# Sum of squares of a head tile: one float32 product against two products of a tile split in two rounded parts

## What is computed

```python
def rmsnorm_2(x, g):
    xf = x.astype(jnp.float32)
    y = xf * lax.rsqrt(jnp.mean(xf * xf, axis=-1, keepdims=True) + EPS)
    return (y * g.astype(jnp.float32)).astype(x.dtype)

# in each of two layers, HEAD_DIM = DIFF_QK_DIM = 64:
h = rmsnorm_2(x, g_attn[l])
proj = jnp.einsum('bsd,dc->bsc', h, w_in[l])
qa, ka, va, qb, kb, vb = jnp.split(proj, offs, axis=-1)
qa = apply_rope(rmsnorm_2(qa.reshape(B, S, SWA_Q_HEADS, HEAD_DIM), qn_a[l]), cos_a, sin_a)
ka = apply_rope(rmsnorm_2(ka.reshape(B, S, SWA_KV_HEADS, HEAD_DIM), kn_a[l]), cos_a, sin_a)
ya = windowed_gqa_sink(qa, ka, va, sink[l])
qb = apply_rope(rmsnorm_2(qb.reshape(B, S, 2 * DIFF_HEADS, DIFF_QK_DIM), qn_b[l]), cos_b, sin_b)
kb = apply_rope(rmsnorm_2(kb.reshape(B, S, 2 * DIFF_HEADS, DIFF_QK_DIM), kn_b[l]), cos_b, sin_b)
yb = diff_attention(...)
```

## Time and profile before

| | |
|---|---|
| median of 3 runs | 2851.36 us (2851.34 to 2852.1) |
| span of the profiled execution | 2849.4 us |
| TensorE (PE), busy | 2816.4 us, 99% |
| weight loads (PEld), busy | 2362.2 us, 83% |
| VectorE (DVE), busy | 1709.0 us, 60% |
| ScalarE (ACT), busy | 1207.7 us, 42% |
| GpSimd (POOL), busy | 59.0 us, 2% |
| granted TensorE clock | 0.999 of full speed over the span |

### The profile page before, as it was taken

The page is one execution under the profiler, slowest core; times in us unless marked ns, Lnnn a source line. Parts: engine busy times, 40 slices in busy tenths (PEclk is TensorE's granted clock), DMA queues, the critical chain, the costliest instruction groups (busy, mean ns, idle before and its releaser), DMA issues.

```text
span 2849.4 us, 36896 instructions
## 1 busy us (share of the span) xinstructions
PE 2816.4 (99%) x14238; PEld 2362.2 (83%) x14238; DVE 1709.0 (60%) x2648; ACT 1207.7 (42%) x1860; POOL 59.0 (2%) x115
## 2 busy tenths in 40 slices
PE   8999999999999999999999999999999999999999
PEld 6998899999999976788888876588888766688887
DVE  5837768754674465447546467865365478765463
ACT  4236645321333384445334346653233455643231
POOL 0000000000000000000000010000000010000000
PEclk9999999999999999999999999999999999999999
DMA  7631023433432120022222232122223321123223
GB/s 289 229 96 30 16 97 107 133 131 100 132 122 72 59 76 16 1 78 97 98 94 99 94 109 70 32 84 99 94 96 106 101 87 49 49 97 105 92 100 103
DMA packets 73486, 266.16 MB, mean 93 GB/s; under 512 B 8816, under 2 KB 11376, under 8 KB 72032
## 3 DMA queue, kind: packets, MB, share of 16 engines
q1 hardware_dynamic: 63360, 230.31, 24.2%
q0 software_dynamic: 9952, 33.50, 3.5%
HBM read 253.55 MB, written 2.10 MB: 90 GB/s over the span
## 4 chain that ended last, share of the span: by engine, by line
PE 92%; DVE 3%; ACT 2%; issue 2%; DMA 0%; SPq 0%; ACTq 0%; DVEq 0%
PE psum L767 76%; PE psum L1142 2%; ACT temps L1419 2%; PE psum L1364 1%; PE psum L1302 1%; DVE row_stats L1988 1%; DVE arena L1988 1%; PE psum L1150 1%; PE psum L1170 1%; PE psum L1247 1%; PE psum L1229 1%; PE psum L1284 1%; PE psum L861 1%; PE psum L860 1%; PE psum L862 1%
## 5 line engine op out<-in xcount | busy, mean ns | idle before, releaser
L767 PE MATMUL psum<-arena_r,w_hi 128*128 128x512 f32 (+1 forms) x7416 | 2006.0, 369 | 2.5 <-DVE arena_r L1988 1.8
L767 PEld LDWEIGHTS psum<-arena_r,w_hi 128*128 128x128 f32 x7416 | 1336.8, 188 | 221.8 <-issue 61.8
L767 PE MATMUL psum<-arena_r,w_lo 128*128 128x512 f32 (+1 forms) x3708 | 1219.2, 364 | 0.0
L1988 DVE TENSOR_TENSOR w_lo<-w_raw,w_hi 128x1024 fp32r<-128x1024 f32 (+4 forms) x377 | 455.3, 1208 | 525.8 <-ACT w_hi L1419 525.2
L767 PEld LDWEIGHTS psum<-arena_r,w_lo 128*128 128x128 f32 x3708 | 682.3, 188 | 82.2
L1419 ACT ACTIVATE w_hi<-w_raw 128x1024 fp32r<-128x1024 f32 (+4 forms) x377 | 392.6, 1042 | 538.0 <-DMA w_raw<-in_weights 537.7
L1419 ACT ACTIVATE temps<-temps 128x512 f32<-128x512 f32 (+2 forms) x208 | 137.2, 662 | 154.9 <-DVE temps L1988 153.0
L1988 DVE SCALAR_TENSOR_TENSOR temps<-psum,vectors,temps 128x511 f32<-128x511 f32 x246 | 151.0, 655 | 63.5 <-ACT temps L1419 61.6
L1419 ACT ACTIVATE arena<-psum 128x768 f32<-128x768 f32 (+2 forms) x166 | 106.7, 647 | 172.3 <-PE psum L767 58.6
L1419 ACT ACTIVATE arena_r<-temps 128x512 fp32r<-128x512 f32 (+1 forms) x103 | 70.7, 687 | 141.1 <-DVE temps L1988 141.1
L1419 ACT ACTIVATE temps<-psum,vectors 128x768 f32<-128x768 f32 (+1 forms) x85 | 75.2, 885 | 118.5 <-PE psum L767 107.2
(11 more groups left out here) (226 smaller groups left out, 2249.4 us busy)
## 6 DMA issues: line engine op xcount, KB each, us to landing
w_raw<-in_weights SPq DMA_DIRECT2D x261, 512.0 KB, 3.3
w_raw<-in_weights SPq DMA_DIRECT2D x64, 704.0 KB, 4.1
arena<-in_ada SPq DMA_DIRECT2D x32, 512.0 KB, 3.6
arena<-in_ada POOLq DMA_DIRECT2D x24, 512.0 KB, 4.6
modulation_weights<-in_ada POOLq DMA_DIRECT2D x24, 512.0 KB, 3.9
arena<-in_ada_first SPq DMA_DIRECT2D x8, 1024.0 KB, 19.4
w_raw<-in_weights SPq DMA_DIRECT2D x32, 256.0 KB, 2.6
modulation_weights<-arena POOLq DMA_DIRECT2D x60, 128.0 KB, 1.9
```

What stands on the lines that cost most here:

```text
L767: last = mm(lin_at(t, segs, slots, upper)[:, s:s + m], w[:, c], x(k, s, m), start=(k == 0 and a == 0), stop=(k == n_k - 1 and a == 2))
L1988: op(*args, **kw).then_inc(*C.out(signal))
```

## The change

In a norm tile the squares are split like other numbers. ScalarE's square stays as it is. ScalarE then copies it into the rounded format (`square_high`, two pieces of 256 columns in the unused positions of temps), signal tail_hi. GpSimd subtracts the high part from the square and writes the low part over the square, in the rounded format (`square_low`), signal tail_lo. TensorE computes the sum by two products in the rounded format with a rounded copy of `blk`, the high part and then the low part, added in PSUM. The rounded views of temps and of the fixed constants are laid over the old ones; the copy of `blk` is made once, early in ScalarE's program.

With it the order moves: in tiles 1 to 8 the tail (of both kinds) stands behind k=6 instead of k=3, ScalarE does the weights (`ahead`) before the roots, and on GpSimd the swap of tile n-1 stands behind the subtract of tile n.

```diff
@@ build @@
+        T = as_loaded.enter_context(nc.sbuf_tensor("temps", [P, 6, NT], F32))
+        CF = as_loaded.enter_context(nc.sbuf_tensor("fixed_constants", [P, C_FIX], F32))
         as_loaded.close()
         AR = sb("arena_r", [P, ARENA], F32R)
         WL = sb("w_lo", [P, RING], F32R)
+        TR = sb("temps_r", [P, 6, NT], F32R)
+        CR = sb("fixed_r", [P, C_FIX], F32R)
         WH = sb("w_hi", [P, RING], F32R)
         X = sb("X", [P, DT, NT])
-        T = sb("temps", [P, 6, NT])
         SQSUM = sb("square_sum", [P, NT])
-        CF = sb("fixed_constants", [P, C_FIX])
...
+        def square_high(n):
+
+            return TR[:, 2 * (n % 2):2 * (n % 2) + 2, NX:NT]
+
+        def square_low(n):
+            return TR[:, n % 2, 0:NX]
@@ gpsimd @@
+            def low_square(n):
+
+                pool.wait_ge(*C.next("tail_hi"))
+                pool.tensor_tensor(halves(square_low(n)), halves(T[:, n % 2, 0:NX]), square_high(n).bitcast(F32),
+                                   ALU.subtract).then_inc(*C.out("tail_lo"))
+
...
                 for n in range(18):
-                    if specs[n].get("rope") is not None:
-                        swap(specs[n]["rope"], MLA_TAILS + 18 * l + n + 1, turned)
+                    if specs[n]["kind"] == "norm":
+                        low_square(n)
+                    if n and specs[n - 1].get("rope") is not None:
+                        swap(specs[n - 1]["rope"], MLA_TAILS + 18 * l + n, turned)
                         turned += 1
@@ tensor @@
-            ident, ones, blk = CF[:, C_ID:C_ID + P], CF[:, C_ONE:C_ONE + P], CF[:, C_BLK:C_BLK + P]
+            ident, ones, blk = CF[:, C_ID:C_ID + P], CF[:, C_ONE:C_ONE + P], CR[:, C_BLK:C_BLK + P].bitcast(F32)
+            blk_r = CR[:, C_BLK:C_BLK + P]
...
                 def tail(n):
 
-                    pe.wait_ge(sems["free_a"], first + n + 1)
                     if n:
                         taken_from(n - 1)
                     if specs[n]["kind"] == "norm":
-                        last = mm(PS[:, 0, :], blk, T[:, n % 2, 0:NX], start=True, stop=True)
+                        pe.wait_ge(*C.next("tail_lo"))
+                        mm(halves(PS[:, 0, :]), blk_r, square_high(n), start=True, stop=False)
+                        last = mm(PS[:, 0, :], blk_r, square_low(n), start=False, stop=True)
                     else:
+                        pe.wait_ge(sems["free_a"], first + n + 1)
                         for t in range(4):
...
-                        if n and k == (3 if p is None else 5):
+                        if n and k == (6 if p is None else 5):
                             tail(n - 1)
@@ scalar @@
             norm(ALL, mod_shift(0, 0), splits=((-1, 1), (0, 2), (5, 3)))
             load_set(SILU_SET)
+            step(CR[:, C_BLK:C_BLK + P], CF[:, C_BLK:C_BLK + P], ACT.Copy, "act_own")
...
                     step(T[:, n % 2, 0:NX], T[:, 2 + n % 2, 0:NX], ACT.Square if specs[n]["kind"] == "norm" else ACT.Copy, "free_a")
+                    if specs[n]["kind"] == "norm":
+                        step(square_high(n), halves(T[:, n % 2, 0:NX]), ACT.Copy, "tail_hi", after=C.at("free_a"))
...
                 for n in range(1, 18):
                     squared(n - 1)
                     p = band_step(n)
+                    ahead()
                     if p is None:
                         tail_root(n - 1)
-                    ahead()
```

More of the change, by code:

```diff
@@ L506, in build @@
             tail_sum tail_rs tail_made rot_in0 rot_in1 kpe_in rope_made down_taken key_taken v_done v_even v_odd up_taken lat_sq lat_sum kpe_squared cn_done kpe_made
-            nm_made e_made p_made tp_done pt_made pv_done factor_made y_scaled y_hi y_done od_made
+            tail_hi tail_lo nm_made e_made p_made tp_done pt_made pv_done factor_made y_scaled y_hi y_done od_made
             lam_in lam_sum lam_exp sub_rs zero_made raw_hi raw_done raw_scaled dve_gate""".split()
```

## The result

The changed kernel takes 2883.55 us (2882.46 to 2884.06, 4 runs) beside 2851.73 for the kernel before (2851.34 to 2852.16, 4 runs): ratio 1.0112, 95% interval 1.01 to 1.0124. Forecast were 2839.4 us. The profiled span is 2881.7 us.

The account below looks back on a forecast made before the run. TensorE, busy 99% of the 2849.4 us span, was taken as the bound. Cheaper tails (-11.7), the first tails' wait (-0.5) and a startup copy (+0.2) gave 2837.4, plus 1.96 outside the span 2839.4 us; range 2838.5 to 2848.

Parts of the forecast that it names:

- What would show it: Signs in the changed kernel's timeline: 1.13 us between w_lo products across a tail, period 5.9, TensorE waiting under 1 us.
- Price of the tail: On TensorE, each of 26 square-sum tails falls from 0.90 to 0.45 us, saving 11.7 us in all.
- Period of a tile: TensorE's time for 24 products and one tail falls from 6.35 us to 5.89.
- The sum: Span 2849.4 - 11.7 - 0.5 + 0.2 = 2837.4 us; with the 1.96 around it 2839.4 us.
- The layer's first tail: TensorE's old wait at each layer's first tail goes and nothing replaces it: 0.5 us gained over two layers.
- The subtract: GpSimd's subtract for the low part takes an estimated 1.4 us, ending a microsecond before the early tails: no cost.
- Rival 1: GpSimd's subtract starved by VectorE's dense runs, tails wait, 21 us lost: 2860 us; chance 0.08 full, 0.08 in part.
- Rival 2: GpSimd's subtract slow by itself: over 2.5 us early tails wait; 2843.6 us at 2.8, 2852 at 3.4; chance 0.05.
- rival 3: ScalarE's extra 0.6 us in the banded-attention tiles ends up on the path, 7.2 us: 2846.6 us; chance 0.04.
- Rival 4: The rounded product in two pieces costs a float32 pass, so nothing is saved: 2851 us; chance 0.03.

Follow-up runs that it names:

- e2: The kernel before with 32 unused bytes per partition in front of w_hi, moving w_hi and all tensors behind it: 2893.33 us.
- e4: The kernel before with only the change's allocation, temps and fixed constants in front of w_hi: 2893.37 us.
- e5: The changed kernel with w_hi directly behind w_lo, at its address in the kernel before: 2839.81 us.
- e15: The changed kernel with w_hi at its old address and the split undone (one float32 product, no copy or subtract), new order kept: 2851.07 us.
- e9: The kernel before with 32 unused bytes between arena and w_lo, so w_lo and w_hi both move against the arena: 2888.72 us.
- e16: The kernel before with w_lo 32 bytes further from the arena and w_hi 256 bytes further: 2904.3 us.
- e13: The changed kernel with w_hi at its old address and the tails of tiles 1 to 8 back behind k=3: 2860.81 us.

## Why the prediction was wrong

**The step that failed** is none of the sum's terms; it is one left out. The prediction begins with the premise that the edit lengthens the kernel only if TensorE has to wait for something new. It follows the work of every engine, keeps the 0.227 us of a rounded product for the whole kernel and puts the moved allocation at nothing without a word. The runs showed a price without any wait: the new place of w_hi cost 42 us in the kernel before (e2, e4) and 43.7 in the changed one (2883.55 against the 2839.81 of e5), on products that the change does not mention; in the two stretches they took 231.5 instead of 226.2 ns and 176.4 instead of 173.0. "What would show it" named waits at the tails and a distance that stays at 1.56 as signs of being wrong; neither came. None of the rivals had this mechanism; the slower one (starvation, 2860 us) had the sign right for a reason that did not occur.

Two slips in the prediction's figures have no effect on its forecast: 24 x 0.227 is 5.45 and leaves 0.90, the value taken, and 0.72 with half of 0.08 is 0.76 and not 0.78.

**The rest held in the main, read in e5.** Its timeline around two tails:

```profile
1653.03 0.39 PE L1248 MATMUL psum<-temps_r,fixed_r 128*128 128x512 f32 x1
...
1658.70 0.39 PE L786 MATMUL psum<-arena_r,w_lo 128*128 128x512 f32 x1
1658.92 0.39 PE L1248 MATMUL psum<-temps_r,fixed_r 128*128 128x512 f32 x1
1659.15 0.39 PE L1249 MATMUL psum<-temps_r,fixed_r 128*128 128x512 f32 x1
...
1659.83 0.39 PE L786 MATMUL psum<-arena_r,w_lo 128*128 128x512 f32 x1
```

- Price of the tail: 1659.83 - 1658.70 = 1.13 us, as forecast (0.68 + 0.45). The moving operand in two pieces costs what a contiguous one does, 1659.15 - 1658.92 = 0.23.
- Period of a tile: 1658.92 - 1653.03 = 5.89 us, as forecast.
- The sum: e5 stands 11.7 us under the kernel before beside it, forecast 12.0, of which the products were 11.7; e15 gives the products 11.3. That the parts agree to some tenths is in part luck, since a ratio here is known to 3 or 4 us.
- The layer's first tail: forecast that the old wait goes and none comes. The weight loads of the two first tails waited 0.6 us for the subtract. Between the w_lo products around this tail lie 1648.04 - 1646.74 = 1.30 us, 0.17 over a tail without a wait; in the kernel before they were 1645.30 - 1643.60 = 1.70, 0.14 over the 1.56. One small wait took the place of the other, and the 0.5 us of this term was not there.

The w_lo products around the first tail in e5, and in the kernel before the one behind it:

```profile
1646.74 0.39 PE L786 MATMUL psum<-arena_r,w_lo 128*128 128x512 f32 x1
...
1648.04 0.39 PE L786 MATMUL psum<-arena_r,w_lo 128*128 128x512 f32 x1
```

```profile
1645.30 0.39 PE L767 MATMUL psum<-arena_r,w_lo 128*128 128x512 f32 x1
```

The subtract, without and with a rotation on VectorE in the same stretch (e5):

```profile
1650.57 1.29 POOL L735 TENSOR_TENSOR temps_r<-temps,temps_r 128x512 fp32r<-128x512 f32 x1 [3.62 <-ACT temps_r L1440]
...
1662.37 1.71 POOL L735 TENSOR_TENSOR temps_r<-temps,temps_r 128x512 fp32r<-128x512 f32 x1 [3.58 <-ACT temps_r L1440]
...
1662.96 1.67 DVE L2012 TENSOR_TENSOR arena<-arena,square_sum 128x512 f32<-128x512 f32 x1
...
1664.82 0.39 PE L1248 MATMUL psum<-temps_r,fixed_r 128*128 128x512 f32 x1
```

- The subtract: 1.4 us estimated, 1.29 alone. It ended 1.2 us ahead of its tail at 1653.03, forecast a microsecond.
- Rival 1: its mechanism is real and its price is not. While VectorE runs a two-input instruction the subtract takes 1.71 us, and VectorE's next one takes 1.67 instead of 0.69: the two hold each other up in turn. Eight of the 26 subtracts, all in steps with a rotation, took 1.53 to 1.72 us, and the others 1.27 to 1.29. The subtract here still ends at 1664.08, 0.7 us ahead of its tail. By the Trainium skill (SBUF — State Buffer, "Who interferes with whom") a VectorE instruction with two SBUF inputs and a GpSimd instruction that reads SBUF exclude each other. The trace agrees with that. It adds that VectorE's run did not starve GpSimd: the longest subtract was 0.4 us over an undisturbed one, which is less than one VectorE instruction of 0.69.
- Rival 2 (2.5 us for the subtract) and rival 3 (ScalarE in the band): not seen, TensorE waits for nothing new there. Rival 4: refuted by 1.13 us.

## What to carry to other kernels

An allocation that is moved is a part of the change: write down which operands of the hot loop change their distance, and compare the start-to-start distance of untouched instructions in a stretch far from the change before explaining anything inside it. In a stream of rounded-format products that alternates two weight tensors against one moving operand, try first to keep all three at the same place modulo 256 bytes, and put new tensors behind them; this is shown only for this kernel's sizes and the shifts in the table. When a chain gets longer, move its consumer first: here the same split is worth 11.7 us with the tail behind k=6 and costs 9.6 us behind k=3, both with w_hi well placed.

## What the runs showed of the hardware that was not expected

- 32 unused bytes per partition in front of one weight tensor slow a TensorE-bound kernel by 42 us of 2851 (1.5%), at full granted clock and without a gap on TensorE; a shift of all tensors by 32 costs nothing, shifts of w_hi by 256, 512 and 20224 bytes cost nothing.
- The cost shows as 4.4 to 6.6 ns more for a product of 512 columns (867 to 859 matmuls in 200 us instead of 884) and 0 to 4.5 ns for one of 384 (1156 to 1127 instead of 1156). Which reads get in each other's way isn't shown: the weight loads have the same recorded duration, 188 ns, before and after. That the load of the next weights meets the stream of the moving operand is an idea that no run shows, and by itself it doesn't fit: in e9 every weight load is off against the arena, and it costs less than e16, where one in three is. The place of w_lo and w_hi to each other has a part in it; why e16 is the worst and why e9 spares the 384-column stage stays open.
- GpSimd's subtract of 128x512 float32 into the rounded format took 1.29 us alone and up to 1.72 us beside VectorE instructions with two SBUF inputs, and such an instruction 1.67 us instead of 0.69.
- A wait in the dense stream cost TensorE more than its length: 1.41 us for a recorded wait of 1.14 (e13).
